# Tile loops of a decoder layer written out with keys per tile, top-k work spread over 44 steps, first attention set between the groups of the fold

## The reference

```
h = rmsnorm(x, g1);  q, k, v, p = split(h @ w_in)            # q, k, v: 4 heads x 128; p: 512
q, k = rope(rmsnorm(q)), rope(rmsnorm(k))                    # per 64-wide component
# differential attention, causal: two score sets per head
s = einsum('bqhcd,bkhcd->bchqk', q, k) * 64**-0.5            # c = 0, 1
pr = softmax(where(k_pos <= q_pos, s, -1e30))
att = rmsnorm(einsum('bhqk,bkhd->bqhd', pr[:, 0] - lam * pr[:, 1], v), subln_g) * (1 - lam_init)
x = x + concat([att, pool_mix(p)]) @ w_out
# PEER: 8 heads x 16 of 128*128 single-neuron experts per row
xn = rmsnorm(x, g2);  qq = (xn @ w_query) as (8 heads, 2 halves, 128)
s2 = einsum('thcd,hcnd->thcn', qq, sub_keys)                 # 128 scores per head and half
top 16 of each half -> 256 sums per head -> top 16 -> 16 expert numbers, gate = softmax
a = gelu(einsum('td,thkd->thk', xn, w_u[eidx])) * gate
x = x + einsum('thk,thkd->td', a, w_v[eidx])
```

## Time and profile before

| | before |
|---|---|
| median of 3 runs | 3858.1 us (3846.58 to 3862.54) |
| profiled execution, first to last instruction | 3875.0 us |
| instructions | 28973 |
| TensorE busy | 3198.9 us (83%), mean granted clock 0.942 |
| VectorE busy | 2232.6 us (58%) |
| ScalarE busy | 1377.8 us (36%) |
| GpSimd busy (issuing gathers) | 1265.5 us (33%) |
| gathers (queue q0) | 1132.53 MB, 78.4% of 16 engines' span |
| first gather issued | 542.22 us |

### The profile page before, as it was taken

How to read it: one execution, slowest core, us unless ns; L and a number is a source line. 1 busy time by engine, 2 the same in 40 slices (tenths; PEclk the granted TensorE clock), 3 DMA queues, 4 the chain that set the end, 5 groups by cost and what they waited for, 6 DMA issues and landing times.

```text
span 3875.0 us, 28973 instructions
## 1 busy us (share of the span) xinstructions
PE 3198.9 (83%) x7958; PEld 1373.5 (35%) x7958; DVE 2232.6 (58%) x5097; ACT 1377.8 (36%) x3852; POOL 1265.5 (33%) x1107
## 2 busy tenths in 40 slices
PE   7997868897888788878887888788878987789755
PEld 3445534332433243324332433243324332333211
DVE  2223455486549654955496549554965495548633
ACT  1221014433433344334333443344344333443222
POOL 0000014343434333434333434333434343334332
PEclk9998869999999999989999999899999999899899
DMA  5225149999999999989998999899999999799999
GB/s 196 76 78 179 49 173 341 361 371 343 351 356 377 338 350 367 367 333 353 358 361 343 353 354 360 327 351 366 366 344 356 354 361 344 276 360 363 306 260 237
DMA packets 184720, 1207.08 MB, mean 312 GB/s; under 512 B 22232, under 2 KB 22616, under 8 KB 46216
## 3 DMA queue, kind: packets, MB, share of 16 engines
q0 software_dynamic: 155648, 1132.53, 78.4%
q1 hardware_dynamic: 28944, 73.30, 5.4%
HBM read 1191.89 MB, written 14.04 MB: 311 GB/s over the span
## 4 chain that ended last, share of the span: by engine, by line
PE 41%; DVE 24%; DMA 19%; ACT 10%; issue 6%; DVEq 0%; POOL 0%; SPq 0%; ACTq 0%; PEldq 0%; POOLq 0%
PE Y L790 22%; DMA big<-in_wuv,idx_c 14%; DVE big L1383 9%; DMA slot<-in_wuv,idx_c 5%; PE S L622 3%; PE Y L547 3%; PE S L547 3%; DVE qpw L1223 3%; PE S L748 2%; ACT work L871 2%; DVE qpw L1220 2%; DVE slot L1383 2%; PE S L728 2%; ACT L957 2%; ACT diag L971 1%
## 5 line engine op out<-in xcount | busy, mean ns | idle before, releaser
L790 PE MATMUL Y<-big,diag 128*128 128x512 f32 (+1 forms) x3540 | 1820.2, 642 | 530.8 <-ACT diag L971 523.0
L516 POOL DMA_INDIRECT big<-in_wuv,idx_c x885 | 1031.8, 1166 | 2014.0 <-PE Y L790 1702.2
L1383 DVE CUSTOM_DVE_ANT_0 big<-big,h2c 128x1024 f32<-128x1024 f32 (+1 forms) x885 | 1082.2, 1226 | 915.8 <-DMA big<-in_wuv,idx_c 829.3
L790 PEld LDWEIGHTS Y<-big,diag 128*128 128x128 f32 (+1 forms) x3540 | 637.4, 194 | 1559.4 <-ACT diag L971 876.0
L957 ACT ACTIVATE gel<-dots 128x1 f32<-128x1 f32 (+1 forms) x1088 | 219.6, 202 | 1748.4 <-DVE dots L1383 1718.7
L790 PE MATMUL Y<-slot,diag 128*128 128x512 f32 (+1 forms) x812 | 415.3, 636 | 59.4 <-ACT diag L971 57.9
L971 ACT ACTIVATE diag<-ident,amp 128x128 f32<-128x128 f32 x1024 | 411.0, 401 | 33.3
L1383 DVE CUSTOM_DVE_ANT_0 slot<-slot,h2c 128x1024 f32<-128x1024 f32 (+1 forms) x203 | 248.7, 1225 | 195.3 <-DMA slot<-in_wuv,idx_c 184.9
L968 ACT ACTIVATE amp<-gel,gate_c 128x1 f32<-128x1 f32 (+1 forms) x1088 | 320.5, 295 | 35.3
L516 POOL DMA_INDIRECT slot<-in_wuv,idx_c x203 | 214.8, 1058 | 328.7 <-PE Y L790 305.9
L748 PE MATMUL S<-big,work 128*128 128x512 f32 x576 | 296.3, 602 | 0.8 <-ACTq L886 0.8
(11 more groups left out here) (174 smaller groups left out, 2026.4 us busy)
## 6 DMA issues: line engine op xcount, KB each, us to landing
big<-in_wuv,idx_c POOLq DMA_INDIRECT x885
big<-in_w_in SPq DMA_DIRECT2D x8, 1024.0 KB, 11.0
big<-in_wqT SPq DMA_DIRECT2D x4, 2048.0 KB, 7.8
big<-in_xT SPq DMA_DIRECT2D x9, 512.0 KB, 3.4
big<-in_x SPq DMA_DIRECT2D x9, 512.0 KB, 4.5
big<-in_mt SPq DMA_DIRECT2D x9, 512.0 KB, 5.1
qp_dram<-big SPq DMA_DIRECT2D x9, 512.0 KB
qpw<-qp_dram SPq DMA_DIRECT2D x9, 512.0 KB
```

The source lines that it names most:

```text
L516: pool.indirect_dma_start(ring[SLOT[k]][0:r, :], None, wuv, bass.IndirectOffsetOnAxis(ap=idx_c[0:r, k:k + 1], axis=0)).then_inc(landed[SLO ...
L790: mm = pe.matmul(Y[0:w, m * 512:(m + 1) * 512], diag[0:r, s * P:s * P + w], ring[s][0:r, D + m * 512:D + (m + 1) * 512], start=(k == 0), s ...
L1383: dot = dve.tensor_tensor_reduce(out=ring[s][0:r, 0:D], in0=ring[s][0:r, 0:D], in1=h2c[0:r, :], scale=1.0, scalar=0.0, op0=ALU.mult, op1=A ...
```

## The change

- The loops over tiles are gone: all eight tiles with their next sets are written out, on TensorE, ScalarE and VectorE. GpSimd's and SyncE's loops stay.
- Set `t` works on `min(t + 1, 8)` blocks of 128 keys: scores, mask, exponentials, combination, flips and values are cut to `keys_of(t)`.
- Heads begin every 9 steps instead of 10. The two exponentials of a head lie in steps 5 and 6 behind its begin, instead of both in 6. The word that the probabilities' buffer is free (`a_used`) comes from ScalarE behind its last copy, instead of from TensorE.
- The 40 parts of the top-k work lie in 44 steps, with a step without a part behind every tenth part. All that follows the attention begins 3 steps earlier, and the choice ends one step later.
- Set 0's steps 0 to 47 lie between the groups of the fold, three behind each, on TensorE and VectorE. The fold's banks are `Y` and `S1`; set 0's scores go to `S0` and its probabilities to another place (`e_first`). `w_out` is scaled after step 47.
- The samples' work begins at step 55 of set 0 instead of 79. Its result goes by `h2c`.

```diff
 class Plan:
-    head0, headw = 1, 10
-    scores, scale, exp = (0, 1, 2, 3), (4, 5), (6, 6)
+    head0, headw = 1, 9
+    scores, scale, exp = (0, 1, 2, 3), (4, 5), (5, 6)
     combine, flip, evac, values = (8, 9), (10, 11, 12), (11, 12, 12), (12, 13, 14, 15)
...
-    top = take[0] + 1
-    gate = top + 4 * TOPU
-    sample0, samplew = take[0], 20
+    top, tops = take[0] + 1, 44
+    gate = top + tops
+    promote = gate + 1
+    sample0, samplew = project + 6, 20
...
+    def choice(cls, k):
+        return [divmod(i, TOPU) for i in range(4 * TOPU) if k == cls.top + i * cls.tops // (4 * TOPU)]
+def keys_of(t):
+    return min(t + 1, LAST) * P
+        def exp_of(c, t):
+            return e_first[c] if t == 0 else [e0, e1][c][:, 0:keys_of(t)]
+        def bank_of(c, t):
+            return S0[:, 512 * c:512 * c + P] if t == 0 else S[c][:, 0:keys_of(t)]
@@ tensor: scores, values, the program
-                w = P if first else 512
-                mm = pe.matmul(S[c][:, m * 512:m * 512 + w], qT[r, h, :], KT3[r, h, m * 512:m * 512 + w],
-                               start=True, stop=True)
+                w = keys_of(t)
+                lo, hi = m * 512, min((m + 1) * 512, w)
+                if lo < w:
+                    mm = pe.matmul(bank_of(c, t)[:, lo:hi], qT[r, h, :], KT3[r, h, lo:hi], start=True, stop=True)
...
                 if u == 0:
-                    pe.wait_ge(t_evac, n(t_evac, 3 if last else 1 if first else 2))
-                    pe.sem_inc(a_used, 1)
+                    pe.wait_ge(t_evac, n(t_evac, (nb + 3) // 4 + (t == LAST)))
...
-            for k in range(PICKS):
-                a_part(k, first=True)
-            n.settle()
-            with pe.Fori(0, LAST - 1):
+            for j in range(GROUPS):
+                fold(j)
+                for k in range(3 * j, 3 * j + 3):
+                    a_part(k, 0)
+            for k in range(3 * GROUPS, PICKS):
+                a_part(k, 0)
+            for t in range(LAST):
                 for k in range(PICKS):
                     g_step(k, P, PICKS)
-                    a_part(k)
-                n.settle()
-            for k in range(PICKS):
-                g_step(k, P, PICKS)
-                a_part(k, last=True)
+                    a_part(k, t + 1)
@@ scalar: the copies of the flips
-                        elif m < 2:
-                            evac(aT[:, m * 512:(m + 1) * 512], T[:, :])
-                        elif last:
-                            evac(exT[0:ROWS8, :], T[0:ROWS8, 0:P])
+                        nb = min(4, blocks_of(t) - 4 * m)
+                        if m < 2 and nb > 0:
+                            evac(aT[:, m * 512:m * 512 + nb * P], T[:, 0:nb * P])
+                        if m == 2:
+                            if t == LAST:
+                                evac(exT[0:ROWS8, :], T[0:ROWS8, 0:P])
+                            act.sem_inc(a_used, 1)
@@ vector: choice and program
-                if at.top <= k < at.top + 4 * TOPU:
-                    top_part(*divmod(k - at.top, TOPU))
+                for q, u in at.choice(k):
+                    top_part(q, u)
...
+            for j in range(GROUPS):
+                fold(j)
+                for k in range(3 * j, 3 * j + 3):
+                    a_part(k, 0)
+            scale_w_out()
...
-            with dve.Fori(0, LAST - 1) as t:
-                g_rest(t, False)
-                turn(t + 1, False)
-                n.settle()
-            g_rest(LAST - 1, True)
-            turn(LAST, True)
+            for t in range(LAST):
+                g_rest(t, t == LAST - 1)
+                turn(t + 1, t == LAST - 1)
```

More of the change, by code:

```diff
@@ L592, in _, with fold @@
             n.settle()
-            for j in range(GROUPS):
+            def fold(j):
                 if j % 4 == 0:
@@ L757, in a_part @@
                     for u in at.head(k, at.scores, h):
-                        scores_of(h, u, last, first)
+                        scores_of(h, u, t)
                     for m in at.head(k, at.flip, h):
-                        flip(m, last, first)
+                        flip(m, t)
                     for u in at.head(k, at.values, h):
-                        values(h, u, last, first)
-                if first:
+                        values(h, u, t)
+                if t == 0 and k == at.project:
+                    pe.wait_ge(wo_ready, n(wo_ready))
+                if t == 0 and k == at.route:
+                    pe.wait_ge(route_w, n(route_w))
+                if t == 0:
                     for g in range(SEQS // GRP):
```

158 lines of the change are left out of this document (77 added, 81 removed).

## The result

The changed kernel takes 3760.2 us (median of 4 runs, 3756.6 to 3764.5) against 3857.1 us for the kernel before (4 runs, 3846.6 to 3862.5). The ratio on record is 0.9727, 95% interval 0.9701 to 0.9752. That is 105 us, the medians lie 97 us apart (a quotient of 0.9749), and 71 were forecast. The profiled execution has a span of 3762.3 us.

What follows compares the result with a forecast made beforehand. Bound: a ring of gather, dot, Gelu and matmul over five buffers, with no engine full. Terms -20 - 52 + 35 - 22 + 3 - 15 = -71 us gave 3787 us from 3858; range 3735 to 3848 us.

Steps and rivals of the forecast that it cites:

- a ring in which lateness counts: Whole span: gather, dot, Gelu and matmul wait on each other over five buffers; no engine is full, TensorE busiest with 83%.
- Turn of the loop: Six jumps back between tiles: removing them saves about 3.4 us each, -20 us, bounds 0 and -48.5.
- not 7.64, because the ring catches up afterwards: VectorE's first dot behind a branch idles 7.64 us on issue; only about 3.4 us of it was counted as lost.
- Fewer keys: Attention steps: smaller sets save 33.5 us on TensorE and 18 us on ScalarE, together -52 us, bounds 0 and -75.
- The split: Exponentials in two steps: extra table loads of 82 us on ScalarE, 1.1 us lateness per head, +35 us, bounds 0 and +82.
- Rival A: Exponentials' extra table loads reach the end in full, costing 82 instead of 35 us: 3834 us, chance 15%.
- Top-k over 44 steps: Top-k steps of each tile: four added plain steps save 2.75 us per tile, -22 us, bounds 0 and -41.
- heads 9 apart: Attention heads closer together: costed at nothing, but +3 us in the last set, between 0 and +10.
- Before the first gather: Start of the kernel: interleaving fold and first set -10 us, earlier sample work -5 us, together -15 us.
- the samples were to hide half of their work under the projection: Ahead of the first gather: the first half of the sample work moves into the projection, -5 us, bounds +5 and -25.
- Rival B: Attention with heads nine apart: VectorE waits for TensorE at every head, 144 us more, 3931 us, chance 5%.
- rival C: Five buffers swallow the two short exponential delays, plain top-k steps bring 5 us per tile: 3734 us, chance 12%.

Runs made afterwards that it cites:

- one pair of runs: Changed kernel with both exponentials of a head in one step again, ratio 0.9673, beside the changed kernel with them split, 0.9727.
- the two pairs: Split against exponentials together, in the changed kernel (0.9727, 0.9673) and in the changed kernel with the fold in one piece first (0.9704, 0.9687).
- the grid: Written-out loop, all keys or fewer, with heads 10 apart and top-k over 40 steps (0.9847, 0.9727) or 9 and 44 (0.9778, 0.9651).
- the fastest version: Changed kernel with the fold in one piece first, both exponentials in one step and samples from the first take step: 3736.4 us, ratio 0.9651.

## Why the prediction was right, and where it was not

The time and the sign held: 3760 us lies in the range, 27 us under the forecast. The bound was read rightly, as a ring in which lateness counts and not busy time. The order of the parts did not hold. The keys and the split were to be the largest, and the turn of the loop was. The terms, one by one:

1. *Turn of the loop*, -20 forecast, -59 measured (18 either way). This is the term that was mis-sized most. The failed step is "not 7.64, because the ring catches up afterwards". It rested on the last tile as a yardstick for a tile entered without a branch. That tile carries the last set with its extra scores from its first steps on, so it is not a clean one: with the loop written out its first 12 steps take 34.8 us and those of the six tiles before 32.1. It also comes behind the loop's exit, with the 1.75 us on issue shown above. A better yardstick was in the trace before: its first tile, which no jump led into, took 34.2 us for the 12 steps. Measured against clean tiles the turn cost 40.0 - 32.1 = 7.9 us, the whole idle time of the earlier trace rows and not half of it, 6 x 7.9 = 47 us. The other 12 us are inside the interval. The traces do show about 3 us per tile beyond the turn, also in tiles that no jump led into, but of the 84 us between the two executions some 25 are their distance from their medians, and that would be as much; no run shows a cause beyond it.
2. *Fewer keys*, -52 forecast, about -38 measured (21 either way, which holds the forecast). The place is right in part: with only the keys added, the attention steps go from 100.0 to 96.9 us per tile and the first tile of two blocks from 374.7 to 361.2 us. The forecast had them rise with the keys over all tiles, and the change's first tile, 368.5 us, is the one that I gave (368), but one of eight blocks takes 371.5 us and not 384. Of these 12.5 us the turn is 4.5 (7.9 less the 3.4 that I had counted).
3. *The split*, +35 forecast; +21 us (19 either way) in one pair of runs and +7 (22 either way) in the other; in the traces of the two pairs the eight tiles are 4 and 12 us longer with the split. The mechanism was right, more loads and two short delays for one long, and the sign is clear of noise in one pair only. The lateness of two steps laid out one after another was too pessimistic by the matmuls that still run under each, 0.3 us at TensorE instead of 1.1. In the text on what would show it I gave 3.9 us between the Gelus. Measured were 5.10 and 4.91, which is the 5.0 of the sum; the step's own 1.1 us was missing in that sentence. Rival A, the loads at full price, is refuted. The loads took 1.28 us each, and again nothing followed them before the activation, so the drain of the Trainium skill ("ScalarE: Activation LUTs", What ACT_TABLE_LOAD costs) does not show in these rows either.
4. *Top-k over 44 steps* and 5. *heads 9 apart*, -22 + 3 forecast. Together they measured -27 and -29 us in the grid. Alone neither could be told from nothing in the loop (8 us, and 0.9825 against 0.9847). In these traces the stage from step 76 falls by 2 us per tile, close to my 2.75. Out of the changed kernel the top-k over 40 steps shows none of it, 148.9 us for the stage against 149.6, so the term's size is not shown.
6. *Before the first gather*, -15 forecast, +3.5 measured. The forecast named 540 us as the point at which this part fails, and 545.8 is beyond it. Two steps failed. The interleaving was to save 10 us and costs 7.6 at the start of the projection. From the fold's first matmul to the projection the changed kernel takes 61.3 us, where I had 53.5. The fold was in my sum with 31.5 us and takes 38.4, since TensorE, halted for VectorE at four flips, runs parts of it at the lower clock. And the sum had no term for the first set's own scores, flips and values, 8.0 us of TensorE in the changed kernel. The waits at the flips were less than my 12 us, 9.3. What did come forward is the first set: without interleaving the projection starts at 381.8 to 385.1 us instead of 391.1. With heads 10 apart (385.1) two things are left that can have done it, the scaling of w_out behind the heads and the fold's other bank. No run separates them, but the trace before points to the first. There TensorE waits for the word that w_out is scaled (`wo_ready`) ahead of the first set's scores, and idles 6.42 us behind the fold, while VectorE is done with the last group at 360.3 us and with w_out at 364.1:

```profile
365.42 0.80 PE L622 MATMUL S<-KT,qpw 64*128 64x128 f32 x4 [6.42 <-PEq L131]
```

With the keys alone added and the fold first, the scores follow the last group without a gap:

```profile
356.45 1.95 PE L619 MATMUL S<-work,big 128*128 128x128 f32 x16
358.33 0.49 PE L634 MATMUL S<-KT,qpw 64*128 64x128 f32 x4
```

And the samples were to hide half of their work under the projection. They only pushed the route products and the top-k back, and VectorE then ended alone.

By the grid the parts come to -59 - 47 - 28 = -134 us for the fastest version (0.9651), and the split, the interleaving and the early samples take 29 us back from it, which gives the 0.9727 of the change. That the forecast's sum came out near is in part luck, since the errors partly cancel. Against it the turn is worth 39 us more, the keys 14 less, the split costs 21 less (taking 14 us), top-k and spacing bring 9 more, and the start 18 less: -71 - 39 + 14 - 21 - 9 + 18 = -108 us, where the ratio gives -105. Rival B can be set aside by the run with heads 9 apart and by the changed kernel's own tiles, none of which before the last set is over 373 us, and rival C is nearer to what was seen of the split than my own term, though one pair of runs holds the forecast's value just inside its interval.

What stays open: whether anything beyond the turn is in the written-out loop, the split's exact price between 0 and 40 us, and how the gain of the top-k and of the spacing is shared between them.

## What to carry to other kernels

Where a ring with a few buffers sets the pace, as here, price a jump back at the whole idle time behind it and take the yardstick from a tile that does the same work. A delay of one engine counts by what the next engine waits more, so read the idle time of the consumer, not the extra busy time. Undoing one part at a time out of the final kernel does not size parts whose effect is near the scatter; a grid of two by two measures each part twice and shows a large interaction, if there is one. Compare the profiled execution with the median of its kernel before reading small differences from a trace. Before work is interleaved to fill an engine, ask whether that engine then waits for another in short pieces. Here its clock fell for part of what followed, and the fold took 38.4 instead of 31.2 us of TensorE.

## What the runs showed of the hardware

- The same 10 us of full TensorE work in the same order was done at the full clock in one execution and at the lower one in another, of a kernel that is the same there (47 and 27 matmul records, granted clock 1.00 and 0.50), behind the same work with the same waits of 1.21 and 2.75 us. On a path that hangs on TensorE alone this moved the first index search by 10.5 us, and with a second such stretch the first gather by 16.
- A turn of a loop over the tiles cost 7.9 us of a five-buffer ring each time, and none came back. Behind each of the six jumps VectorE idled 7.2 to 8.5 us and ScalarE 5.2 to 5.8 us on issue; at the loop's exit, without a jump, VectorE idled 1.75 us.
- Behind 2.10 us of idle time the same group of 16 matmul records took 3.19 us in one place (granted clock 0.57) and 1.95 us in another.
- 64 more table loads of 1.28 us, 82 us more of ScalarE, made the kernel longer by 21 us in one pair of runs and 7 in another (some 20 either way).
